# A hybrid decoder layer on one core: the input projection by one level of Strassen's scheme, in two phases of 1024 tokens

## What is computed

```python
xn = _rmsnorm(x, g_pre)
u = xn @ w_in
gq, gk, gv, gg, glr, dq, dk, dv, dg, ga, gb = jnp.split(u, cuts, axis=-1)
log_a = jax.nn.log_sigmoid(glr @ w_gla_lr + b_gla_lr) / GLA_TAU
o_a, s_new = _gla(q, k, v, log_a, gla_s0)            # gated linear attention, recurrent over the tokens
y_a = (rmsnorm(o_a) * silu(gg)) @ w_gla_branch
for g, (win, dil) in enumerate(((128, 1), (512, 4), (2048, 16))):
    o_g, lse_g, nbuf = dilated_window(dq[g], dk[g], dv[g], ...)
y_b = (sum over g of softmax(lse)[g] * o_g * silu(dg)) @ w_dil_branch
merged = sigmoid(ga) * y_a + sigmoid(gb) * y_b
h = x + _rmsnorm(merged @ w_out, g_post)
h = h + (pe @ w_ple_proj) * sigmoid(h @ w_ple_gate)
```

## Time and profile before

| | |
|---|---|
| median of three runs | 2802.43 us |
| the profiled execution: span, first to last instruction | 2799.7 us |
| the profiled execution's own time | not given; the fastest run is 2.6 us above this span, the median 2.7 us |
| busy TensorE / VectorE / ScalarE / GpSimd | 2769.4 / 1077.3 / 861.5 / 360.3 us |
| projection of the last token tile ends at | about 2154 us |

### The profile page before, as it was taken

The page is one execution under the profiler, slowest core; times in us unless marked ns, Lnnn a source line. Parts: engine busy times, 40 slices in busy tenths (PEclk is TensorE's granted clock), DMA queues, the critical chain, the costliest instruction groups (busy, mean ns, idle before and its releaser), DMA issues.

```text
span 2799.7 us, 40580 instructions
## 1 busy us (share of the span) xinstructions
PE 2769.4 (99%) x16108; PEld 1453.6 (52%) x16108; DVE 1077.3 (38%) x2401; ACT 861.5 (31%) x1728; POOL 360.3 (13%) x601
## 2 busy tenths in 40 slices
PE   8999999999999999999999999999999899999998
PEld 4444456555545665666555555555544344444444
DVE  6211134444333443344223333333322655555452
ACT  5111124444312222333123321111112544444441
POOL 2000011111311002120011113222100000000000
PEclk9999999999999999999999999999999999999999
DMA  9543464655577566584576789787646966556642
GB/s 283 134 168 132 147 208 152 214 177 207 190 253 286 187 195 213 185 273 152 179 278 208 257 234 301 239 249 252 216 152 224 277 172 174 148 149 180 164 112 58
DMA packets 326542, 558.35 MB, mean 199 GB/s; under 512 B 179114, under 2 KB 184305, under 8 KB 321874
## 3 DMA queue, kind: packets, MB, share of 16 engines
q1 hardware_dynamic: 268722, 290.57, 34.9%
q0 software_dynamic: 43376, 231.63, 25.3%
q10 hardware_dynamic: 14256, 33.56, 3.3%
HBM read 378.70 MB, written 236.79 MB: 220 GB/s over the span
## 4 chain that ended last, share of the span: by engine, by line
PE 96%; DMA 1%; SPq 1%; DVE 1%; ACT 0%; issue 0%; POOL 0%; DVEq 0%; POOLq 0%
PE out L2654 40%; PE out L2214 22%; PE out L2651 18%; PE out L1143 2%; PE out L1128 2%; PE out L2657 2%; PE out L1134 1%; PE out L615 1%; PE out L626 1%; PE out L625 1%; PE out L1429 1%; PE out L1389 1%; DMA mix_pe_in<-in_p_prompt 1%; SPq L356 1%; PE out L1117 1%; PE out L1402 0%
## 5 line engine op out<-in xcount | busy, mean ns | idle before, releaser
L2654 PE MATMUL out<-w_hi,xn_hi 128*128 128x512 f16 x1792 | 679.9, 379 | 1.0 <-DVE w_lo L2514 0.5
L2654 PE MATMUL out<-w_lo,xn_hi 128*128 128x512 f16 x1792 | 679.4, 379 | 0.0
L2654 PE MATMUL out<-w_hi,xn_lo 128*128 128x512 f16 x1792 | 679.4, 379 | 0.0
L2545 ACT ACTIVATE stage<-out 128x512 f32<-128x512 f32 (+1 forms) x170 | 99.4, 585 | 926.9 <-PE out L2654 613.2
L2592 DVE TENSOR_SCALAR stage<-out 128x512 f32<-128x512 f32 (+1 forms) x170 | 114.7, 675 | 645.0 <-PE out L2654 398.4
L2651 PE MATMUL out<-xn_hi,w_hi 128*128 128x512 f16 x768 | 291.3, 379 | 0.0
L2651 PE MATMUL out<-xn_hi,w_lo 128*128 128x512 f16 x768 | 291.1, 379 | 0.0
L2651 PE MATMUL out<-xn_lo,w_hi 128*128 128x512 f16 x768 | 291.1, 379 | 0.0
L2654 PEld LDWEIGHTS out<-w_hi,xn_lo 128*128 128x128 f16 x1792 | 175.4, 98 | 211.5 <-issue 0.3
L2654 PEld LDWEIGHTS out<-w_hi,xn_hi 128*128 128x128 f16 x1792 | 175.8, 98 | 192.6 <-issue 6.2
L2654 PEld LDWEIGHTS out<-w_lo,xn_hi 128*128 128x128 f16 x1792 | 175.4, 98 | 186.4 <-issue 0.3
(11 more groups left out here) (320 smaller groups left out, 3950.5 us busy)
## 6 DMA issues: line engine op xcount, KB each, us to landing
out<-in_cache_kv_w POOLq DMA_DIRECT2D x64, 1020.0 KB, 9.8
U<-stage SPq DMA_DIRECT2D x224, 256.0 KB, 4.6
raw<-in_w_in SPq DMA_DIRECT2D x78, 512.0 KB, 5.1
UT<-stage SPq DMA_DIRECT2D x96, 256.0 KB, 4.2
sw_kc<-in_cache_kv_w ACTq DMA_DIRECT2D x24, 1024.0 KB, 9.6
sw_vc<-in_cache_kv_w POOLq DMA_DIRECT2D x24, 1024.0 KB, 9.4
sw_rows<-U POOLq DMA_DIRECT2D x32, 512.0 KB, 7.8
out<-in_cache_kv_w POOLq DMA_DIRECT2D x16, 1008.0 KB, 8.0
```

Source lines behind the costliest of these rows:

```text
L2545: move_out(act, m, lambda o, x: act.activation(o, x, ACT.Copy, scale=1.0 / W_SCALE))
L2654: last = pe.matmul(out[m % 3][:, :], x[:, k, at:at + P], y[:, k, :], start=first, stop=final)
```

## The change

Each column tile of 512 is now made for 1024 tokens by one level of Strassen's scheme (the form with 7 products and 15 sums): the depth, the tokens and the columns are halved, and 7 products of halves (`P1, P6, P2, P7, P4, P5, P3`) take the place of 8. Tokens come in pairs: token tile j with token tile j + 4 of the phase. For each pair the seven operands (halves of x and four sums of them, made by GpSimd in `Inputs.sum`) are kept transposed in `xf`. Seven operands of 1024 tokens take about the room that all 2048 tokens took, so the 20 column tiles are run twice: phase 0 for tokens 0 to 1023 and the samples, phase 1 for tokens 1024 to 2047. The operands of phase 1 are prepared during the first column tiles, kept in DRAM (`XB`) and loaded at the turn. `w_in` is read twice.

One generation G is one column tile in one phase (40). It has two halves D, each 128 of the 256 tokens or columns of a half block, of 7 products of 24 matmuls of 256 columns, one after another, each in one of three banks. ScalarE moves P1 out, and VectorE adds the others into `stage`, seven additions of 128 x 512 for a half. The seven weight operands of the next generation are cut one by one into their single buffers as the last product that read them ends. Their four sums (128 x 1024 f32) are made by GpSimd, for G = 0 by VectorE. A generation has 8 + 9 slots in phase 0 and 10 + 10 in phase 1, 740 in all. The prompt's linear attention is run in two parts, 8 chunks in each phase (every 6 and every 7 slots), the sample windows move to slot 236, the prompt's windows to phase 1. The samples' row buffers (`sw_rows`) are 2 and not 3. The low-rank columns are made once in each phase. The first two pairs are transposed by TensorE (56 transposes), the others and the samples by DMA (rows of 7 x 512).

```diff
+PAIRS = 4
+FORMS = 7
+P1, P6, P2, P7, P4, P5, P3 = range(FORMS)
+STEPS = 3 * HALF_K
+PRODUCT_BANKS = 3
+PARTS = ((8, 9), (10, 10))
+SUM_AT = (1, 1)
+HI_AT = ((3, 6, 6, 7, 9, 10, 10), (2, 5, 5, 6, 8, 9, 10))
+LO_AT = ((4, 7, 7, 8, 10, 11, 12), (3, 6, 6, 7, 9, 10, 11))
-GLA_SLOT, GLA_PERIOD = GLA_TILES * TILE_SLOTS + 4, 6
-WINDOW_SLOTS = [277, 351, 452]
-SAMPLE_SLOT, SAMPLE_PERIOD = 527, 15
-CUT_SLOT, CUT_PERIOD = 170, 10
+GLA_SLOTS, GLA_PERIODS = (GLA_TILES * TILE_PARTS[0] + 4, 625), (6, 7)
+SAMPLE_SLOT, SAMPLE_PERIOD = 236, 15
+WINDOW_SLOTS = [409, 481, 547]
+CUT_SLOT, CUT_PERIOD = 95, 4
...
+    def cut_hi(self, act, G, f):
+        if f in (P1, P2, P3):
+            act.wait_ge(self.raw_loaded[0 if f == P1 else 1], 16 * (G + 1))
+        else:
+            act.wait_ge(self.sum_ready, 4 * G + {P7: 1, P6: 2, P4: 3, P5: 4}[f])
+        wait(act, self.made, used_count(G, f))
+        act.activation(self.w[0][f][:, :, :], self.sources[f], ACT.Copy, scale=W_SCALE).then_inc(self.hi_ready, 1)
+    def cut_lo(self, dve, G, f):
+        dve.wait_ge(self.hi_ready, FORMS * G + f + 1)
+        dve.scalar_tensor_tensor(out=self.w[1][f][:, :, :], in0=self.sources[f], scalar=W_SCALE, in1=self.w[0][f][:, :, :],
+                                 op0=ALU.mult, op1=ALU.subtract).then_inc(self.lo_ready, 1)
+    def sum(self, eng, G, f):
...
+        if f == P6:
+            eng.wait_ge(self.lo_ready, FORMS * G + P1 + 1)
+            eng.wait_ge(self.sum_ready, 4 * G + 1)
+            eng.tensor_tensor(self.sources[P6], self.sources[P1], self.sources[P7], ALU.subtract).then_inc(self.sum_ready, 1)
...
+    def add(self, dve, D, f, us, out, other):
+        return dve.scalar_tensor_tensor(out=out, in0=self.shaped(D, self.product(D, f, us), us), scalar=1.0 / W_SCALE, in1=other,
+                                        op0=ALU.mult, op1=ALU.add)
+    def vector(self, dve, q):
...
+            if f == P5:
+                dve.wait_ge(self.made, made_count(D, P5, us))
+                dve.wait_ge(self.dve_kept, DVE_COUNT[D, P4, us])
+                self.add(dve, D, P5, us, c01, c01)
+                self.add(dve, D, P5, us, c11, c11).then_inc(self.dve_kept, 1)
...
+    def pool(self, pool, q):
+        for H, phase, at in self.coming(q):
+            if at == SUM_AT[phase]:
+                self.sum(pool, H, P7)
+            for f, lower in ((P6, P1), (P4, P2), (P5, P7)):
+                if at == LO_AT[phase][lower]:
+                    self.sum(pool, H, f)
...
+    def multiply(self, pe, G, d, f, us, step):
+        u, step = us[step // STEPS], step % STEPS
+        k, i = divmod(step, 3)
+        x, w = self.xf[(0, 0, 1)[i]], self.w[(0, 1, 0)[i]][f]
...
+        out = self.bank[TURN_OF[2 * G + d, f, us] % PRODUCT_BANKS][:, u * HALF:(u + 1) * HALF]
...
+        return pe.matmul(out, x[:, 2 * d + u, f * HALF_K + k, :], w[:, k, :], start=start, stop=stop)
...
+    def load_pairs(self, sp, d):
+        sp.wait_ge(self.made, made_count(2 * COLUMN_TILES - 2 + d))
+        for j in (2 * d, 2 * d + 1):
             for s in range(2):
+                sp.dma_start(self.xf[s][:, j, :, :].rearrange("p n t -> p (n t)"), self.XB[j, s]).then_inc(self.pair_loaded[j], 16)
...
+            projection.sum(dve, 0, P7)
+            for f in range(FORMS):
+                projection.cut_lo(dve, 0, f)
+                if f in (P1, P2, P7):
+                    projection.sum(dve, 0, {P1: P6, P2: P4, P7: P5}[f])
+                inputs.keep_lo(dve, 0, f)
+                if f == P2:
+                    for i in inputs.tiles(1):
+                        inputs.scale(dve, i)
```

More of the change, by code:

```diff
@@ new lines, in length, with part, ended @@
+def length(f, us):
+    return 2 * STEPS if f == SAMPLE_STEP else STEPS * len(us)
+def part(D, c):
+    order, parts = products(D), PARTS[D // (2 * COLUMN_TILES)][D % 2]
+    total, at, pieces = sum(length(*turn) for turn in order), 0, []
+    low, high = total * c // parts, total * (c + 1) // parts
+    for turn in order:
+        a, b = max(low - at, 0), min(high - at, length(*turn))
+        if a < b:
+            pieces.append((*turn, a, b))
+        at += length(*turn)
+    return pieces
+def ended(q):
+    G, d, c = place(q)
+    return [(f, us) for f, us, _, b in part(2 * G + d, c) if b == length(f, us)]
@@ L247, in has @@
[L247 to L260, removed]
+                (self.rstd_ready, n), (self.scaled, n), (self.summed, self.sums_before(self.PREPS)), (self.turned, units), (self.hi_ready, units),
@@ new lines, in source, with turn @@
+    def source(self, k, f):
+        kind, *at = self.SOURCES[f]
+        if kind == "s":
+            return self.sums[k % 2][:, at[0], :]
+        return self.tile(self.tiles(k)[at[0]])[:, at[1] * BANK:(at[1] + 1) * BANK]
+    def turn(self, pe, k, f):
+        n = k * FORMS + f
+        bank = self.bank[n % len(self.bank)]
+        pe.wait_ge(self.scaled, self.tiles(k)[1] + 1)
+        if self.SOURCES[f][0] == "s":
+            pe.wait_ge(self.summed, self.sums_before(k + 1))
+        wait(pe, self.lo_ready, n + 1 - len(self.bank))
+        src = self.source(k, f)
+        for b in range(HALF_K):
+            last = pe.transpose(bank[:, b * P:(b + 1) * P], src[:, b * P:(b + 1) * P], self.identity[:, :])
+        last.then_inc(self.turned, 1)
@@ L1205 @@
     EVERY = 2
-    RING = 3
+    RING = 2
     FIRST = 1
@@ L2370, in side_queue @@
+            for phase in range(PHASES):
+                prompt_gla.queue(q, slot - GLA_SLOTS[phase], phase)
             sample_gla.queue(q, slot - GLA_SAMPLE_SLOT)
@@ L2453, in _ @@
             pool.memset(empty[:, :, HD:HD + 1], -MASKED).then_inc(empty_ready, 1)
-            for t in range(4, TOKEN_TILES):
-                inputs.norm(pool, t)
-            cutter.start(pool)
+            for k in range(inputs.SAMPLE + 1):
+                for i in inputs.tiles(k):
+                    inputs.norm(pool, i)
+                inputs.sum(pool, k)
             def shift(b, g, i):
@@ L2674, in _ @@
+                projection.tensor(pe, q)
+                for phase in range(PHASES):
+                    lowrank.tensor(pe, phase, q - LOWRANK_SLOTS[phase], inputs, projection)
+                for phase in range(PHASES):
+                    prompt_gla.tensor(pe, q - GLA_SLOTS[phase], phase)
                 for g in range(GROUPS):
```

1380 lines of the change are left out of this document (852 added, 528 removed).

## The result

The changed kernel takes 2911.27 us (median of 4 runs, 2904.35 to 2914.29), the kernel before 2803.56 us beside it: ratio 1.0381, 95% interval 1.0366 to 1.0396. It is slower by 108 us, where 68 us less were forecast; the forecast missed by 176 us and lies outside its range. The profiled execution took 2904.35 us with a span of 2902.2 us.

The account below looks back on a forecast made before the run. TensorE was taken to bound the kernel from end to end: 2799.7 - 193 + 13 + 47 + 16 + 30 + 8 + 6 + 5 = 2731.7 us, with 2.7 us to the median 2734, stated as 2735; range 2690 to 2790 us.

Parts of the forecast that it names:

- Main matmuls, 193 us: Projection on TensorE: 7680 matmuls of 512 columns become 13440 of 256 at 0.1091 us each, gaining 193 us.
- The rival that a matmul isn't halved: Main matmuls: weight load and stream don't overlap wholly, so nothing is gained, about 2928 us; 3 in 100.
- Windows, +30 us: Prompt's window steps: 2.93 us each, with VectorE's late products and cuts costing 30 us over 202 slots.
- The rival that was to be the slow case: Window steps: VectorE's queue makes each 0.7 us longer, 141 us in place of 30, 2846 us; 15 in 100.
- Tail and turn: Later products and phase change: tail's own idle of 18 us stays; loading xf at the turn costs 6 us (0 to 15).
- The lock: VectorE and GpSimd in SBUF: one waits for the other's instruction; seven cuts meeting sums lose 1.5 us a generation.
- the start's 11 us and the 5 of generations 1 and 2: Early generations: the only time charged for GpSimd's sums holding VectorE, 16 us lower if only GpSimd waits.
- Cuts well over 1.22 us: VectorE's cuts: the forecast took 1.22 us each and called itself wrong if they last well over that.
- Linear attention, +16 us: Prompt's linear attention: VectorE's additions queue behind the chunk's work, 1 us lost in each of 16 chunks (0 to 50).
- The start, +47 and +5 us: First generation: ends at about 100 us, +47 us (25 to 75); generations 1 and 2 lose 5 us to sums.
- Sample windows, +8 us (0 to 30): Sample windows: two row buffers give loads three slots of some 3 us against 7.8 us to land, costing 8 us.
- a rival worth 10 in 100: Start and DMA cost twice: transposes at 17 us a pair, xf and row loads late, 2794 us; 10 in 100.

Follow-up runs that it names:

- experiment 1: Changed kernel with GpSimd's 156 weight-block sums cut to 128x8 from the second generation on (projection values wrong): 2847.05 us, ratio 1.0156.
- experiment 4: Changed kernel with x of the last four token pairs loaded eight slots ahead of preparation in place of four: 2896.49 us, ratio 1.0335.
- experiments 10 and 11: Changed kernel with the four corrections (2786.44 us): pair-preparation steps further apart, 2790.07 us; then also second pair's scale and third pair's row cuts earlier, 2785.34 us.
- experiment 6: Changed kernel with sample windows at three slots a row step, 17 a sample, first sample's values loaded 14 slots earlier: 2868.35 us, ratio 1.0236.
- The four corrections: Each alone on the changed kernel: x loaded earlier 2896.49, weight cuts set apart 2875.24, sample windows paced 2868.35, last group's rows in 16 pieces 2877.46 us.
- experiment 12: Changed kernel with x early, cuts apart, sample windows paced, rows in pieces, pair steps apart, start reordered, GpSimd's sums 128x8 (values wrong): 2758.64 us, ratio 0.9836.

## Why the prediction was wrong

- *Main matmuls, 193 us.* Right: 0.1092 us each where nothing disturbs them. The rival that a matmul isn't halved is out.
- *Windows, +30 us.* Too high. A step takes 116.40 / 40 = 2.91 us against the 2.93 of its own sum, with no wait. The rival that was to be the slow case didn't come; VectorE's list paces nothing there.
- *Tail and turn.* The tail is idle for 8.7 us in place of the 18 that the prediction kept; the turn showed 11.5 us only once the stage before it no longer waited.
- *The lock: the step that failed.* Its size on the cuts was right. The prediction had 1.5 us a generation; the cuts measure (1455 - 1221) x 280 = 66 us, 1.6 a generation. It left out VectorE's other instructions: with the small sums VectorE was busy 90 us less in all. And apart from the start's 11 us and the 5 of generations 1 and 2 it was priced at nothing, since VectorE was not the bound and "covered". It was not: taking the weight sums away gave 64 us of time. In the linear attention, where VectorE's list holds the additions, the chunk and the cuts in strict order, lateness reached TensorE almost undiminished: 42.5 us less of VectorE's busy time came with 39.7 us less time, of the 59 by which the span shrank. In the generations between, only half of it did (41 us and 19). How much of the 64 us is the hold, and how much that the sums themselves are shorter, stays open. The guess of seven cuts meeting sums at random also missed that the order in the code makes the meeting: the cut of P2 starts the sum, and the next cut is P7's. The Trainium skill's page that was cited, SBUF — State Buffer, "Who interferes with whom", has the exclusion in both directions; the row at 1703.54 agrees: a VectorE cut waited for a GpSimd sum. Its warning was dismissed by the step above, not by a row. Cuts well over 1.22 us were one of the prediction's own signs of being wrong, and that sign came.
- *Linear attention, +16 us.* Too low, for that reason: experiment 1 alone took 40 us from its two stages.
- *The start, +47 and +5 us.* Too low by 41. The first generation ended at 116 us, forecast 100. The first three are 61 + 39.4 + 39.4 + 8 (low-rank products) = 148 us of work, and they ended at 241.4 us: 93 us lost, against 52. Taking GpSimd's pair sums away gave 16.5 us, loading `x` earlier 10 (the fourth generation's start in experiment 4); the rest is a chain over four engines, which experiments 10 and 11 shortened by little. What exactly holds it stays open.
- *Sample windows, +8 us (0 to 30).* Mis-sized, outside its own bounds: experiment 6 took 43 us away. The prediction had seen the pace, three slots of 3 us against 7.8 us to land, and priced it by the median. Eight samples each end with a flip that waits for the last of four such loads, and in the first sample that load stood behind 3.25 MB of values in GpSimd's queue: VectorE was idle 18.6 us for it.
- *Missing from the sum: the last group's rows*, 34 us. No term had them. In the changed kernel's schedule 8 MB of copies stand just ahead of the first loads of the last window group in one queue, where the kernel before had them just behind. "Row loads late" stood in a rival worth 10 in 100, but for the sample stage.
- *The clock: missing altogether.* Every wait was priced at its length. Of the 283 us between 2902.2 and the 2799.7 - 180 of work alone, 212 are idle and 71 are busy time more, an estimated 60 of them from half clock; the granted clock was 0.962 on average and matmuls in its lower stretches started 0.21 us apart.

The four corrections (15, 36, 43, 34 us) and the pair sums (20) with what the small weight sums gave beyond the cuts set apart (64 - 36 = 28) make 176 us, as much as the miss. That it fits to a microsecond is chance, as the forecast already held 112 us of waits and the parts overlap. Run together, with the two steps on the start, they gave 2911 - 2759 = 153 us (experiment 12), and that kernel is still 24 us above the forecast. Its span of 2758.9 us holds 139 us above the 2619.7 of work alone. What makes up all of them stays open.

## What to carry to other kernels

When the bounding engine gets faster, price every stall of the others anew in the stages where they work in strict order: "the engine is 60% busy" covers nothing there. Here 42.5 us of VectorE's time in the linear attention went with 39.7 us of the whole, but in the other stages 41 us with 19. Look at which instruction releases a GpSimd operation and what the other engine does next; the two meet by construction, not by chance. And check each large transfer in the new schedule: loads with two buffers need a pace that their landing allows, and small loads must not stand behind megabytes in one queue. Four such rearrangements turned 3.8% slower into 0.6% faster without changing the work.

## What the runs showed of the hardware

- A single wait of 3.2 us ended with the clock at half: TensorE idle until 127.47 us, 0.50 granted from 126.5 to 133.2. One of 3.3 us at 182.6 us did not. The kernel before, with hardly any wait, had 0.998 on average; this one 0.962, and 0.79 in its first generation.
- GpSimd's 128x512 sum of two SBUF inputs takes 1.27 us alone and 2.12 to 2.25 us when VectorE's cuts run one after another; its 128x1024 sum takes 2.35 us. Both directions of the hold are in the traces, and it isn't the cuts alone that are held: the linear attention's scan took 1541 ns on average beside the sums and 1217 with small ones.
- 16 copies of 512 KB spread over 96 slots ran beside the window loads with no wait, the first two of them in a generation with a DMA share of 0.92. As two of 4 MB ahead of a 1 MB load in the same queue the load landed after 40 us; issued behind such a load, in the kernel before, they left it to land after 11.3 us.
